# A hybrid encoder trunk: reordering the first pointwise projection of the convolution module, starting the filter on one chunk, and moving eight filter taps to VectorE

## The reference

```python
def conformer_conv_module(h, pw1_w, pw1_b, dw_w, dw_b, ln_g, ln_b, pw2_w, pw2_b):
    u = h @ pw1_w + pw1_b                      # (256, 1024) @ (1024, 2048)
    a, gate = jnp.split(u, 2, axis=-1)
    u = a * jax.nn.sigmoid(gate)
    u = lax.conv_general_dilated(              # causal, depthwise, 31 taps
        u, dw_w[:, None, :].astype(u.dtype),
        window_strides=(1,), padding=[(CONV_WIDTH - 1, 0)],
        dimension_numbers=("NWC", "WIO", "NWC"),
        feature_group_count=D_MODEL) + dw_b
    u = jax.nn.silu(layernorm(u, ln_g, ln_b))
    return u @ pw2_w + pw2_b                   # added to x by the caller
```

## Time and profile before

| | us |
|---|---|
| median of 3 runs | 1392.22 (1392.02 to 1392.23) |
| the profiled execution | 1391.96 |
| its span | 1390.2 |
| TensorE busy | 1367.1 |
| VectorE busy | 1176.8 |
| ScalarE busy | 984.3 |

### The profile page before, as it was taken

The page is one execution under the profiler, slowest core; times in us unless marked ns, Lnnn a source line. Parts: engine busy times, 40 slices in busy tenths (PEclk is TensorE's granted clock), DMA queues, the critical chain, the costliest instruction groups (busy, mean ns, idle before and its releaser), DMA issues.

```text
span 1390.2 us, 20436 instructions
## 1 busy us (share of the span) xinstructions
PE 1367.1 (98%) x6683; PEld 1131.9 (81%) x6683; DVE 1176.8 (85%) x1391; ACT 984.3 (71%) x1247; POOL 92.2 (7%) x123
## 2 busy tenths in 40 slices
PE   9999999999999999999999999999999999999997
PEld 7885888888887888888888888888888888888885
DVE  3993666667768998999999899999989999999997
ACT  3174544455667788877878887787888888778885
POOL 1000000002223000000000000000000000000000
PEclk9999999999999999999999999999999999999999
DMA  9602665555638999999999999999999999999992
GB/s 291 227 27 84 206 195 185 189 197 161 202 99 306 394 395 367 394 394 362 367 394 394 335 393 394 356 374 394 395 333 395 395 352 381 395 383 341 395 395 104
DMA packets 197230, 428.97 MB, mean 309 GB/s; under 512 B 7263, under 2 KB 44255, under 8 KB 197182
## 3 DMA queue, kind: packets, MB, share of 16 engines
q1 hardware_dynamic: 192510, 412.79, 81.0%
q0 software_dynamic: 4512, 15.51, 4.0%
q10 hardware_dynamic: 160, 0.04, 0.0%
HBM read 419.67 MB, written 8.65 MB: 308 GB/s over the span
## 4 chain that ended last, share of the span: by engine, by line
PE 91%; DVE 4%; ACT 3%; issue 1%; DMA 0%; ACTq 0%; DVEq 0%; POOL 0%; POOLq 0%
PE bank L1153 70%; PE bank L1202 6%; PE bank L1084 4%; PE bank L1204 3%; PE bank L1104 2%; PE bank L1138 2%; PE bank L1451 2%; DVE wl L1654 2%; ACT wh L778 1%; ACT prob L858 0%; PE bank L1010 0%; DMA R<-in_conv_ln_b 0%; ACT both L925 0%; PE bank L1355 0%; PE bank L1094 0%
## 5 line engine op out<-in xcount | busy, mean ns | idle before, releaser
L1654 DVE TENSOR_TENSOR wl<-ring,wh 128x1024 fp32r<-128x1024 f32 x758 | 907.7, 1223 | 68.5 <-ACT wh L778 23.7
L778 ACT CAST wh<-ring 128x1024 fp32r<-128x1024 f32 x758 | 789.5, 1056 | 167.5 <-PE bank L1153 167.5
L1153 PE MATMUL bank<-wh,both 128*128 128x512 f32 (+1 forms) x1888 | 583.6, 391 | 0.9 <-DVE wl L1654 0.7
L1153 PEld LDWEIGHTS bank<-wh,both 128*128 128x128 f32 x1888 | 349.0, 188 | 72.3 <-DVE wl L1654 2.8
L1153 PE MATMUL bank<-wl,both 128*128 128x512 f32 (+1 forms) x944 | 366.4, 388 | 0.0
L1153 PEld LDWEIGHTS bank<-wl,both 128*128 128x128 f32 x944 | 177.2, 188 | 37.0
L1153 PE MATMUL bank<-wh,ath 128*128 128x512 f32 x512 | 201.1, 393 | 0.8
L1153 PE MATMUL bank<-wl,ath 128*128 128x512 f32 x512 | 199.6, 390 | 0.0
L1153 PE MATMUL bank<-wh,atl 128*128 128x512 f32 x512 | 199.4, 389 | 0.0
L1202 PE MATMUL bank<-both,wh 128*128 128x512 f32 x352 | 124.7, 398 | 1.4 <-DVE both L1683 1.1
L1153 PEld LDWEIGHTS bank<-wh,ath 128*128 128x128 f32 x512 | 96.1, 188 | 23.5 <-DVE wl L1654 3.8
(11 more groups left out here) (254 smaller groups left out, 880.8 us busy)
## 6 DMA issues: line engine op xcount, KB each, us to landing
ring<-in_moe_w_gate SPq DMA_DIRECT2D x112, 1024.0 KB, 7.6
ring<-in_moe_w_up SPq DMA_DIRECT2D x112, 1024.0 KB, 7.9
ring<-in_moe_w_down SPq DMA_DIRECT2D x112, 1024.0 KB, 8.0
ring<-in_conv_pw_w SPq DMA_DIRECT2D x12, 1024.0 KB, 11.0
ring<-in_ffd_w_gate SPq DMA_DIRECT2D x11, 1024.0 KB, 5.4
ring<-in_ffd_w_up SPq DMA_DIRECT2D x11, 1024.0 KB, 5.4
ring<-in_ffd_w_down SPq DMA_DIRECT2D x11, 1024.0 KB, 4.8
ring<-in_w_q SPq DMA_DIRECT2D x4, 1024.0 KB, 5.0
```

Source lines behind the costliest of these rows:

```text
L778: sa.copy(wh[:, place(n, h), :], ring_half(n, h)).then_inc(wh_ready, 1)
L1153: mm = pe.matmul(out_bank, lhs, rhs, start=start and n == 0, stop=stop and n == 2, **kw)
L1654: ve.tensor_tensor(wl[:, place(n, h), :], ring_half(n, h), wh[:, place(n, h), :].bitcast(F32), ALU.subtract).then_inc(wl_ready, 1)
```

## The change

Seven edits that belong together:

1. The projection goes chunk by chunk: value half of a chunk, gate half of the same chunk, then the next. Each half has a bank of its own, all eight banks in turn (`mix_bank`). A new semaphore `pair_done` tells ScalarE that the even chunk's gate half is done; the odd chunk's is told by the units used, as before.
2. `params_T` stands after the value half of chunk 0.
3. VectorE's list begins with 17 taps of chunk 0 alone, then alternates between neighbouring chunks (0 and 1, 1 and 2, 2 and 3, 3 and 4), and ends with the rest and chunk 5's share alternating. Gates stand before taps 0, 17, 45, 65, 95 (two) and 122 (two).
4. `SHARED_TAPS` goes from 12 to 4: TensorE has 4 taps of chunk 5, VectorE 27. TensorE has 66 taps and not 74, VectorE 182 and not 174.
5. TensorE's filter now uses banks that hold the halves of chunks 5 and 7, and waits for six gates before chunk 5's taps and for all eight before those of chunks 6 and 7.
6. The bias goes to `xg_rows`, a tile that nothing uses this early. GpSimd issues it when the first half of x is in, ahead of its first two roots.
7. VectorE adds the bias right after it has made its part of `hT`, ahead of copying the tap rows.

```diff
-SHARED_TAPS = 12
+SHARED_TAPS = 4
+LEAD_TAPS = 17
+ALONE = 125 + SHARED_TAPS
...
 def vector_taps():
 
-    order = [(c, w) for w in range(CONV) for c in (0, 1)]
-    for i in range(CONV):
-        order += [(2, i), (3, i)]
-        if 7 <= i < 7 + SHARED_TAPS:
-            order.append((4, i - 7))
-    return order + [(c, w) for w in range(SHARED_TAPS, CONV) for c in (4, DVE_CHUNKS)]
+    order = [(0, w) for w in range(LEAD_TAPS)]
+    at = LEAD_TAPS
+    for c in range(4):
+
+        pairs = CONV - at
+        for i in range(pairs):
+            order += [(c, at + i), (c + 1, i)]
+        at = pairs
+    order += [(4, w) for w in range(at, CONV)]
+    rest = order[ALONE:]
+    shared = [(DVE_CHUNKS, w) for w in range(SHARED_TAPS, CONV)]
+    order = order[:ALONE]
+    for pair in itertools.zip_longest(rest, shared):
+        order += [tap for tap in pair if tap]
+    return order
...
-        pw2_bias = R3[:, 0:1024]
+        pw2_bias = xg_rows[:, :]
...
+        def mix_bank(c, g):
+
+            return PB[4 * (c % 2) + 2 * g + c // 2 % 2][:, 0:S]
...
+            pool.wait_ge(x_in[0], 16)
+            pool.dma_start(pw2_bias, spread(conv_pw2_b, 0, P)).then_inc(pw2b_in, 16)
             for t in range(TT):
                 root(0, t)
 
             pool.wait_ge(cv_T, 2)
-            pool.dma_start(pw2_bias, spread(conv_pw2_b, 0, P)).then_inc(pw2b_in, 16)
...
-                product_done(sa, U_PW1 + 2 * (c // 2) + 1)
+                if c % 2 == 0:
+                    sa.wait_ge(pair_done, c // 2 + 1)
+                else:
+                    product_done(sa, U_PW1 + c)
...
-                for g in range(2):
-                    n = U_PW1 + 2 * j + g
-                    if n == U_PW1 + 1:
-                        params_T()
-                    landed(pe, n)
-                    w = slot(n).rearrange("p (k f) -> p k f", k=8)
-                    if j >= 2:
-
-                        pe.wait_ge(glu_ready, 2 * (j - 2) + 2)
-                    for c in range(2):
+                if j >= 2:
+
+                    pe.wait_ge(glu_ready, 2 * (j - 2) + 2)
+                for c in range(2):
+                    for g in range(2):
+                        n = U_PW1 + 2 * j + g
+                        if j == 0 and c == 0 and g == 1:
+                            params_T()
+                        if c == 0:
+                            landed(pe, n)
+                        w = slot(n).rearrange("p (k f) -> p k f", k=8)
                         for k in range(DC):
-                            if n == 0 and c == 0:
+                            if n == U_PW1 and c == 0:
                                 h_ready(0, k)
-                            mm = pe.matmul(PB[2 * g + j % 2][:, c * S:(c + 1) * S], w[:, k, c * P:(c + 1) * P],
-                                           hT[:, k, :], start=(k == 0), stop=(k == DC - 1))
-                    consume(mm)
+                            mm = pe.matmul(mix_bank(2 * j + c, g), w[:, k, c * P:(c + 1) * P], hT[:, k, :],
+                                           start=(k == 0), stop=(k == DC - 1))
+                        if c == 1:
+                            consume(mm)
+                        elif g == 1:
+                            mm.then_inc(pair_done, 1)
...
                 if w == 0:
-                    pe.wait_ge(glu_ready, c + 1)
+                    pe.wait_ge(glu_ready, 6 if c == DVE_CHUNKS else DC)
...
             norm_out(0, hT, CV_MIX0)
+            ve.wait_ge(pw2b_in, 16)
+            ve.wait_ge(unit_high, TT)
+            for t in range(TT):
+                ve.tensor_tensor(X[:, t, :], X[:, t, :], pw2_bias, ALU.add).then_inc(x_biased, 1)
             ve.wait_ge(cv_T, 2)
...
-            ve.wait_ge(pw2b_in, 16)
-            ve.wait_ge(xT_done, 4)
-            for t in range(TT):
-                ve.tensor_tensor(X[:, t, :], X[:, t, :], pw2_bias, ALU.add).then_inc(x_biased, 1)
             ve.wait_ge(cv_ready, 2)
...
             glu(0)
-            glu(1)
-            ve.wait_ge(glu_ready, 2)
-            glu_before = {32: (2, 3), 68: (4, 5), 98: (6, 7)}
+            glu_before = {17: (1,), 45: (2,), 65: (3,), 95: (4, 5), 122: (6, 7)}
```

More of the change, by code:

```diff
@@ L14 @@
 from contextlib import ExitStack
+import itertools
 import numpy as np
@@ L287, in trunk @@
         sig_ready = sem("sig_ready")
+        pair_done = sem("pair_done")
         glu_ready = sem("glu_ready")
@@ L730, in _ @@
                     make_taps(tap_list[8:DIAGS])
-                product_done(sa, U_PW1 + 2 * (c // 2) + 1)
+                if c % 2 == 0:
+                    sa.wait_ge(pair_done, c // 2 + 1)
+                else:
+                    product_done(sa, U_PW1 + c)
                 if c >= 2:
                     sa.wait_ge(glu_ready, c - 1)
-                sa.activation(sig[:, c % 2, :], PB[2 + c // 2 % 2][:, (c % 2) * S:(c % 2 + 1) * S], ACT.Sigmoid,
+                sa.activation(sig[:, c % 2, :], mix_bank(c, 1), ACT.Sigmoid,
                               bias=cv[:, CV_PW1B + DC + c:CV_PW1B + DC + c + 1]).then_inc(sig_ready, 1)
@@ L1575, in glu @@
                 ve.wait_ge(sig_ready, c + 1)
-                ve.scalar_tensor_tensor(out=upad[:, c, CONV - 1:], in0=PB[c // 2 % 2][:, (c % 2) * S:(c % 2 + 1) * S],
+                ve.scalar_tensor_tensor(out=upad[:, c, CONV - 1:], in0=mix_bank(c, 0),
                                         scalar=cv[:, CV_PW1B + c:CV_PW1B + c + 1], in1=sig[:, c % 2, :],
```

## The result

| | us | ratio to before, 95% interval |
|---|---|---|
| before | 1392.22 median (1391.47 to 1393.42, 11 runs) | |
| changed | 1395.65 median (1394.44 to 1396.18, 11 runs) | 1.0023 [1.0015, 1.0030] |
| changed, profiled execution | 1395.9, span 1394.1 | |

The change makes the kernel 3.4 us slower. Of the changed kernel's single times four lie at 1394.4 to 1394.5 and seven at 1395.6 to 1396.2; the profiled execution is one of the seven, and its own sum is somewhat larger than the median's. Every execution also has its mean granted TensorE clock on record: 0.997 of full speed in each of the four, 0.996 in each of the seven. A thousandth of 1394 us is 1.4 us, the distance between the two groups (an estimate, as the means are rounded).

The account below looks back on a forecast made before the run. TensorE bounds the kernel, VectorE about 1 us behind. Saving 3.46 against waiting 3.76 gives +0.30; early transfer +0.4; sum +0.7 on 1391.96 is 1392.7, median 0.26 above: 1392.9 us, range 1391.0 to 1396.0.

Parts of the forecast that it names:

- the rival that was given 0.28: TensorE's clock falls in the new wait for the last gates: +2.35 to +4.0 us, centre 1395.4, chance 0.28.
- the case that was given 0.50: The forecast case: saving paid back as waiting, clock kept, small early-transfer cost; 1391.9 to 1394.0, chance 0.50.
- The saving, the projection, the reach of the taps: On TensorE: eight taps less save 3.46 us, projection keeps 256 records, taps reached at 67.15 as before.
- The wait: TensorE, after chunk 5's four taps end at 68.88, waits 3.76 us for VectorE's last gates, until 72.64.
- the lead: VectorE's opening 17 taps of chunk 0 alone, each waiting for the one before: 0.51 us from start to start.
- the count of 110 equal steps: VectorE from glu(1) to glu(6): 105 taps and 5 gates, 110 starts at 0.3955, 43.50 us less 0.26.
- The clock: TensorE's clock around the wait: the forecast case kept it, with taps behind the wait 0.216 us apart.
- The price of 1.65 to 3.3: Loss if TensorE's clock falls: 3.3 us at half pace lose 1.65; twice that long loses 3.3.
- The early transfer: The early 512 KB bias competes with first weights: pushes up to 1.6 us, tap-row wait up to 0.5, parameters 0 to 1.6.
- the term of 0.4: Cost taken in all for the early bias transfer, between nothing and 2.1 us, shifting TensorE and VectorE alike.
- The order on VectorE: VectorE's last gates are what is late: with glu(7) 3.8 us earlier the saving would be whole.
- VectorE's own end: VectorE's last tap ends at 96.2, where it ended at 100.46, so its chunks are there before TensorE's means.

Follow-up runs that it names:

- e8: e2 with GpSimd issuing the bias after its two roots, not ahead of them: 1388.67 us, ratio 0.9976 to the kernel before.
- e6: The changed kernel with the last two gates before tap 117, not 122: 1392.82 us, ratio 1.0004 to the kernel before.
- e4: The changed kernel with the bias issued and added in its old places: 1401.13 us, ratio 1.0061 to the kernel before.
- e9: The kernel before with SHARED_TAPS 4 instead of 12, all else old: 1396.27 us, ratio 1.0030.
- e5: The changed kernel with the last two gates before tap 119, not 122: 1394.12 us, ratio 1.0014 to the kernel before.
- e2: The changed kernel with the last two gates before tap 111, not 122: 1389.28 us, ratio 0.9979 to the kernel before.
- e3: The changed kernel with SHARED_TAPS back at 12, eight taps back on TensorE: 1393.28 us, ratio 1.0007 to the kernel before.
- e10: e8 with SHARED_TAPS 3 and the last gates before tap 110: 1388.27 us, ratio 0.9975 to the kernel before.
- e1: The changed kernel with 14 identity products on TensorE in its wait for the last gates: 1393.02 us, ratio 1.0007 to the kernel before.
- e7: The kernel before with the early bias alone (other tile, early issue, early adds): 1392.00 us, ratio 1.0000.

## Why the prediction was right or wrong

The forecast was 1392.9, in the range of 1391.0 to 1396.0. The time came out at 1395.65, inside it, but by the rival that was given 0.28 and not by the case that was given 0.50. That rival's centre was 1395.4.

*The saving, the projection, the reach of the taps:* right. TensorE arrives at 66.90 (put at 67.15), four taps take 1.73, and with both waits gone the full saving shows (e8, 3.43 below the kernel before).

*The wait:* the mechanism was right, the size 0.63 short: 4.39 from the end of the four taps to the restart, put at 3.76. 0.25 is TensorE's earlier arrival: its front ran 0.34 earlier instead of later. 0.14 is the lead: taps that wait for the one before are 0.52 apart, not 0.51. Another 0.25 are two places that the count of 110 equal steps missed. Where the list goes from one pair of chunks to the next, and no gate happens to stand between, two taps of the same chunk follow each other. The chain of the changed kernel shows them with 0.48 where the others have 0.40:

```profile
54.22 0.48 DVE R L1611
...
66.13 0.48 DVE R L1611
```

*The clock:* the step that failed. The forecast case put the clock's cost at nothing; it was 2.98. I had the row with the fall 2.6 us after the last matmul, had a wait longer than that, and still put the kept clock first, because the matmuls before the wait were dense. The changed kernel and e6 show that dense work on both sides doesn't protect: in e6 it fell with TensorE already working again. That the time fell inside the stated range is owed to the range, which took in most of the rival. The rule of the Trainium skill that the prediction quoted ("TensorE: Matmul & The Clock Gate", "Why this matters for your kernels") was on this side: the traces of the changed kernel, e4, e6 and e9 agree that an idle gap between bursts can put the clock back, and the profiled execution of e5, with 3.04 us idle and the clock at 1.00, shows that it need not. The price of 1.65 to 3.3 held, 2.98 in the changed kernel and 1.7 in e6, though the rows that it was taken from don't show it: at the start of the kernel the granted clock reads 1.00 throughout and the pace is 5 records against 7, not half. They fit the low stretches of these runs roughly: TensorE works through 5.6 us of it in the changed kernel (73.0 to 78.6) and 3.4 in e6, at half pace.

*The early transfer:* the mechanism was right for the tap rows and wrong for the parameters. The rows landed at 5.74 + 8.2 = 13.9 and not 13.0; TensorE lost 0.1 to them in the profiled execution, 0.4 in e2 and 1.17 in e3, in a place where 0.5 had been the most. In e3 the tap rows were issued later too, at 6.60, since SyncE's issue of the transfer before them took 3.75 us. The prediction had no term for this: that issue took 2.85 to 3.75 in the twelve traces, with the early bias and without it, and what held it isn't shown. The parameters were not late. The tap transposes start 3.6 us behind the first projection record in e4, e8 and e10, and 3.6 to 4.9 behind it in the six kernels of the new order with the early bias, 0.3 later in the mean. So the term of 0.4 was near in size, half by luck. By the Trainium skill ("DMA: Bandwidth & Descriptors", "Queues, rings and completion order"), quoted in the prediction, each DMA engine goes round between the queues that it has work for. The trace agrees in that the bias did not stand behind weights issued before it, as these rows of the changed kernel show:

```profile
xg_rows<-in_conv_pw_b POOLq DMA_DIRECT2D x1, 512.0 KB, 7.0
...
ring<-in_conv_pw_w SPq DMA_DIRECT2D x1, 1024.0 KB, 11.1
```

The bias, issued at 4.45, is there at 11.5, before the gate unit that was issued at 2.18 and lands at 13.3.

*The order on VectorE:* the sum said that glu(7) 3.8 us earlier would make the saving whole, and e2 is that kernel, but for its wait of 0.40 for the tap rows. *VectorE's own end:* put at 96.2, found at 96.74.

## What to carry to other kernels

Work moved off the bound engine is worth nothing until the engine that now feeds it delivers in time, and what counted here was the place of the one operation waited for, not the sum of the work. A wait on TensorE is to be priced with its length and with the clock behind it: 4.2 us of waiting cost 7.2 here. If it can't be removed, filling it with products that nobody reads can win the second part back, 2.6 us in e1.

## What the runs showed of the hardware that was not expected

The clock can fall after TensorE has started again, as in e6, at 72.5 for a restart at 71.11, and a wait of 3.04 may leave it alone (e5). So a wait's length doesn't tell whether it costs the clock. The same is found where no change was made. In e7, whose code from the means on is that of the kernel before, TensorE idles 0.43 and 1.12 us around eight small transposes, and takes up work again with this record:

```profile
141.38 0.67 PE L1203 MATMUL bank<-both,wh 128*128 128x512 f32 x1 [1.12 <-DVE both L1684]
```

The clock falls there and stands at 0.63 in the mean of the stretch from 142 to 146. The profiled execution of the kernel before has the same two gaps, and no fall:

```profile
141.67 0.50 PE L1202 MATMUL bank<-both,wh 128*128 128x512 f32 x1 [1.12 <-DVE both L1683]
```

By 147 to 149 us, where both reach the same four small products (147.33 before, 148.67 in e7), e7 has lost 1.6 us: 1.34, and the 0.29 that it was ahead. Its profiled execution is 1393.62, 1.6 above its median. The records of single executions bear this out. Of the 74 executions of the kernel before that were timed beside the experiments, the six slowest, 1392.97 to 1393.88, are just those with a mean granted clock of 0.997 or 0.996; the other 68, 1390.92 to 1392.74, have 0.998 or 0.999. So the upper end of that kernel's spread goes with a fallen clock. Where it falls in them is shown by no trace of that kernel, and what decides whether it falls stays open.
